# Second convolution layer of a five-layer block: low weight parts made by adding transfers instead of GpSimd subtractions

## The chip, the core and the metric

The kernel runs on one NeuronCore of a Trainium2 chip. The metric is the device time of one execution in microseconds. The engines are TensorE (PE; its weight loads are listed as PEld), VectorE (DVE), ScalarE (ACT), GpSimd (POOL) and SyncE (SP, which issues most transfers). They run their own instruction streams and meet at semaphores. TensorE runs at 1.2 or 2.4 GHz; the profile shows the granted clock as a share of the higher level.

## What is computed

512 tokens of width 1024 in float32 pass through four mixer layers and then a block of two attentions and a feed-forward. Layers 0 and 3 are the same convolution mixer with different weights; layer 3 is "the second convolution layer" (index `j = 1` in the code).

```
def conformer_conv_mixer(h, w_in, conv_w, conv_b, ln_g, ln_b, w_out):
    proj = h @ w_in                                  # 1024 -> 3 * 2048
    val, glu_gate, z = jnp.split(proj, 3, axis=-1)
    u = val * jax.nn.sigmoid(glu_gate)
    u = causal_depthwise_conv(u, conv_w) + conv_b    # 31 taps
    u = jax.nn.silu(layer_norm(u, ln_g, ln_b))
    return (u * jax.nn.silu(z)) @ w_out
...
mix = (sigmoid(gate_a) * (o_a @ w_branch_a) + sigmoid(gate_b) * (o_b @ w_branch_b))
x = x + mix @ w_out
```

The last two lines are from the attention block; `w_branch_a` and `w_branch_b` are the branch weights of the text.

## The kernel before

**Products.** A float32 product is made of three matmuls of a shorter format (float32r): high part of the weights with high part of the activations, high with low, and low with high. `HH` and `HL` hold the parts of the activations, `WH` and `WL` those of the weights. One product of 128 output columns (`gemm`) is 8 x 3 = 24 matmuls of 128x128 by 128x512.

**Weight chunks.** All weights come in a fixed list of chunks `specs` of up to 1 MB. `load_chunk` (SP) loads chunk i from HBM into a raw buffer, half of `WR`; `split_hi` (ACT) copies each of its two halves, 128 partitions x 1024, to `WH`, which rounds them; `split_lo` (POOL) subtracts, `WL = WR - WH`. `WH` and `WL` have two buffers, so `split_hi` of chunk i waits until PE is done with chunk i-2, and `load_chunk` waits until the low parts of the chunk that had the raw buffer are made. PE waits for the low part of a half (`w_lo`) before its product. A chunk of two runs of 128 columns lies in the buffer as eight strips of 256 columns, each half being eight strips of 128.

**Convolution layer.** `layer_a_tensor`, `_vector`, `_scalar` and `_gpsimd` run 33 slots. In slots 0 to 15 PE makes the gate product (half 1 of the slot's chunk) and then the value product (half 0); in slots 16 to 28 one z product, so that a chunk lasts two slots. In slot s ACT first splits the chunk of slot s+1, then takes the sigmoid of the gate; DVE multiplies value and gate and then runs 16 (later 8) of the 31-tap accumulations into PSUM (`SCALAR_TENSOR_TENSOR ps<-AR,CW,ps`). Four channel tiles are convolved wholly or partly by products on ACT and additions on POOL (`TENSOR_TENSOR AR<-AR`). `conv_plan` deals the taps and additions to the slots. On POOL the split of chunk s+1 stands in slot s ahead of the slot's additions, behind those of the slot before. Of `specs`, the layer has 16 chunks with value and gate, 8 with z and 8 of `w_out`.

**Attention block.** While the pairs of attention heads run, the gate products 0 to 13 pass through one staging tile, `STAGE`, which lies in one of the raw buffers together with probabilities of a pair (`W_FREE`), and go to HBM by `gates_sync`; they come back by `gates_back_sync` and ACT takes their sigmoid. The 8 gate chunks (from `C_GATE`) use only the other raw buffer. The first branch chunk is `C_BR`. After the last gate product (n = 15) ACT copies the attention outputs into `HH` (`s_ohi`), POOL and DVE make `HL` from them, even ones and odd ones (`s_olp`, `s_olv`), and PE starts on the branch weights; DVE makes the odd ones after it has waited for the whole product 15.

Of the kernel before, what the change touches and what calls it, by code (L numbers as in the profile page):

```python
# [51 lines left out]
class Engine:  # L52
# [65 lines left out]
def build_program(nc, x, a_norm, a_w_in, a_conv_w, a_conv_b, a_ln_g, a_ln_b, a_w_out, b_norm,  # L118
# [4 lines left out]
    with ctx:  # L123
# [106 lines left out]
        def layer_a_chunks(j):  # L230
# [3 lines left out]
            for i in range(KE // 2):  # L234
                cols(a_w_in[j], (2 * E + 256 * i, 256), used=(a_z, j, 2 * i + 1))
# [49 lines left out]
        def slot_of(i):  # L285
            return (C_GATE + 1) % 2 if C_GATE < i < C_BR else i % 2

        def raw_slot(i):
            return WR[:, slot_of(i) * 2048:(slot_of(i) + 1) * 2048]

        def halves(tile, i):
# [14 lines left out]

        def load_chunk(sp, i):
# [4 lines left out]
            if before:  # L312
                sp.wait_ge(w_lo, before[-1], len(halves(WR, before[-1])) - 1)
            if i == C_BR:
                sp.wait_ge(u_t, 11, 0, 1)
                sp.wait_ge(s_gout, 13)
            if kind in ("in", "deep"):
# [5 lines left out]
                for n, (c0, width) in enumerate(runs):  # L323
                    sp.dma(dst[:, :, o:o + width], src[:, :, c0:c0 + width]).then_inc(
# [29 lines left out]
        def gemm(pe, i, half, o, gen, last=None):  # L354

            pe.wait_ge(w_lo, i, half)
# [10 lines left out]
        def gemm_tokens(pe, i, part, tb, o, gen):  # L367
            sl = slice(tb * P, (tb + 1) * P)
            for n in range(2):
                pe.wait_ge(w_lo, i, n)  # L370
# [176 lines left out]
        def project_tensor(pe, p, first):  # L547
# [10 lines left out]
            def wait_tile(k):  # L558
                pe.wait_ge(w_lo, c0 + k // 2, k % 2)
# [1114 lines left out]
        s_pe, s_pek, s_c, s_cst, s_gelu, s_ck = (sig(n) for n in ("s_pe", "s_pek", "s_c", "s_cst", "s_gelu", "s_ck"))  # L1674
        s_cs, s_cp, s_cexp, s_ct, s_cev = (sig(n) for n in ("s_cs", "s_cp", "s_cexp", "s_ct", "s_cev"))
        u_s, u_ttr, u_exp, u_sh, u_t, u_ev = (sig(n) for n in ("u_s", "u_ttr", "u_exp", "u_sh", "u_t", "u_ev"))
        u_shp, u_fill, s_gout = sig("u_shp"), sig("u_fill"), sig("s_gout")
# [160 lines left out]
        def compress_tensor(pe, n, src):  # L1838
            w3, src3 = t3(W1[n], 16), t3(src, 2)
            if n == 0:  # L1840
# [4 lines left out]
                op.then_inc(s_pe)  # L1845
# [8 lines left out]
        def compress_rest_tensor(pe, n):  # L1854
            pe.wait_ge(s_pek, n, 15)
            if n:
                pe.wait_ge(s_cst, 0)
            pe.mm(banks[5][:, 0:1], PES[n], ones[:, 0:1], True, True).then_inc(s_c, n, "rest")

        def compress_vector(dve):  # L1860
            dve.wait_ge(s_pe)
# [16 lines left out]
        def compress_rest_vector(dve, n):  # L1878
            dve.wait_ge(s_c, n, "rest")
            dve.copy(small(1, "cst", n), banks[5][:, 0:1]).then_inc(s_cst, n)  # L1880

        def compress_rest_scalar(act, n, *dst):
            for at, (g, o) in enumerate(dst):
                act.wait_ge(s_cst, n)
# [5 lines left out]
        def compressed_tensor(pe, i):  # L1890
            pe.wait_ge(s_ck, 1)
# [99 lines left out]
        def pair_scores_vector(dve, u, i, e):  # L1991
# [6 lines left out]
            elif u.n == 2:  # L1998
                dve.wait_ge(s_ct, 3)
                dve.wait_ge(s_c, "v")  # L2000
                dve.wait_ge(w_lo, C_GATE, 1)
            bias = u.bias[e][:, 0:n][:, ::-1]
            if u.n >= 8 and i:
                dve.wait_ge(u_fill, u.n, i, e)
# [4 lines left out]
        def pair_fill_gpsimd(pool, u):  # L2009

            pool.wait_ge(s_tab[1 if u.n < 10 else 2])
            for i, e in BLOCKS:
                if i:
# [4 lines left out]
                        u_fill, u.n, i, e)  # L2018
# [51 lines left out]
        def pair_weigh_tensor(pe, u, i):  # L2070
# [10 lines left out]
            for m in (1, 0) if i == 1 else (i,):  # L2081
                o = [u.bank[rows_of(e), m * P:(m + 1) * P] for e in range(2)]
                if u.branch == 0:
                    pe.wait_ge(s_ck, 1)
# [12 lines left out]
        def second_tensor(pe):  # L2097
# [45 lines left out]
            pe.wait_ge(s_cst, 1)  # L2143
# [594 lines left out]
```

## Time and profile before

| | us |
|---|---|
| median of 3 runs | 2710.47 |
| lowest, highest | 2709.81, 2712.2 |
| the profiled execution | 2709.93 |
| its span | 2708.2 |
| PE busy in the span | 2598.6 (96%) |
| VectorE busy | 1572.4 (58%) |
| ScalarE busy | 1111.8 (41%) |
| GpSimd busy | 1526.1 (56%) |

Times inside the execution are microseconds from the start of the span. The second convolution layer runs from about 1480 to 1910 us, its slots 0 to 28 from about 1501 to 1790; the branch weights come at about 2240. Of the chain of work that ended last, PE holds 75% and VectorE 17%.

### The profile page before, as it was taken

The numbers are of one execution on the slowest core, as the hardware profiler recorded it, in microseconds if no ns is written. First come the engines' busy times: TensorE is split into PE (matmuls) and PEld (weight loads), VectorE is DVE, ScalarE is ACT, GpSimd is POOL, SyncE is SP. The second block draws the span as 40 slices with busy tenths as digits, with TensorE's granted clock in tenths as the row PEclk, the third lists the DMA queues.
The fourth block names the chain that finished last, engine by engine and source line by source line (L and its number), as shares of the span: only waits on it lengthen the run. The fifth ranks groups of instructions, "written<-read, shape, count | busy, mean of one in ns | idle before, by whom it ended". The sixth has DMA issues, their size and how long they took to land.

```text
span 2708.2 us, 31509 instructions
## 1 busy us (share of the span) xinstructions
PE 2598.6 (96%) x12172; PEld 2094.6 (77%) x12172; DVE 1572.4 (58%) x2509; ACT 1111.8 (41%) x1787; POOL 1526.1 (56%) x846
## 2 busy tenths in 40 slices
PE   8999799999999999999999999989999999999998
PEld 6777687877777777888888777768877677788887
DVE  4999975135865834444441799987488753432202
ACT  3454444334654633222232455444335544332322
POOL 3798856444444355444454589866634537544652
PEclk9999999999999999999999999989999999999999
DMA  4232223544344222333333223122431223232221
GB/s 120 78 91 70 89 70 81 102 95 65 77 78 67 78 78 78 109 94 94 101 101 94 63 78 94 63 77 94 117 109 51 95 94 117 82 109 94 94 105 51
DMA packets 267541, 236.63 MB, mean 87 GB/s; under 512 B 16181, under 2 KB 240655, under 8 KB 267392
## 3 DMA queue, kind: packets, MB, share of 16 engines
q1 hardware_dynamic: 264240, 223.94, 29.9%
q0 software_dynamic: 3152, 10.68, 1.3%
q8 instruction: 97, 1.59, 0.2%
q14 instruction: 52, 0.43, 0.1%
HBM read 228.75 MB, written 5.84 MB: 87 GB/s over the span
## 4 chain that ended last, share of the span: by engine, by line
PE 75%; DVE 17%; ACT 3%; issue 2%; POOL 2%; DMA 1%; DVEq 0%; POOLq 0%; ACTq 0%; SPq 0%
PE ps L64 72%; DVE ps L81 7%; DVE AR L81 4%; PE ps L67 2%; DVE AR L73 2%; DVE HL L81 1%; ACT L70 1%; ACT AR L70 1%; POOL AR L73 1%; POOL WL L73 1%; ACT HT L70 1%; DVE X L73 1%; DVE ST L97 0%; DMA AR<-in_x 0%; POOL HL L73 0%
## 5 line engine op out<-in xcount | busy, mean ns | idle before, releaser
L73 POOL TENSOR_TENSOR WL<-WR,WH 128x1024 fp32r<-128x1024 f32 (+1 forms) x405 | 1006.9, 2508 | 863.9 <-ACT WH L70 863.9
L64 PE MATMUL ps<-HH,WH 128*128 128x512 f32 x3080 | 1231.8, 400 | 29.7 <-POOL WL L73 15.1
L64 PE MATMUL ps<-HH,WL 128*128 128x512 f32 x3080 | 1207.3, 392 | 0.0
L64 PE MATMUL ps<-HL,WH 128*128 128x512 f32 x3080 | 1206.7, 392 | 0.0
L64 PEld LDWEIGHTS ps<-HH,WH 128*128 128x128 f32 x3080 | 583.4, 189 | 174.8 <-issue 40.8
L64 PEld LDWEIGHTS ps<-HL,WH 128*128 128x128 f32 x3080 | 583.6, 189 | 123.4 <-issue 6.7
L64 PEld LDWEIGHTS ps<-HH,WL 128*128 128x128 f32 x3080 | 582.6, 189 | 123.6
L70 ACT ACTIVATE WH<-WR 128x1024 fp32r<-128x1024 f32 (+1 forms) x405 | 403.9, 1046 | 477.0 <-PE ps L64 455.4
L81 DVE SCALAR_TENSOR_TENSOR ps<-AR,CW,ps 128x512 f32<-128x512 f32 x732 | 504.8, 747 | 10.4 <-ACT ps L70 3.0
L70 ACT ACTIVATE AR<-ps 128x512 f32<-128x512 f32 (+3 forms) x265 | 132.4, 523 | 413.7 <-PE ps L64 314.2
L73 DVE TENSOR_TENSOR AR<-AR 128x512 f32<-128x512 f32 (+1 forms) x161 | 226.5, 1436 | 39.3 <-ACT AR L70 37.6
L64 PE MATMUL ps<-AR 128*64 128x128 f32 (+16 forms) x1458 | 222.7, 349 | 17.6 <-DVE AR L81 7.3
L73 POOL TENSOR_TENSOR AR<-AR 128x512 f32<-128x512 f32 x154 | 204.8, 1347 | 32.1 <-ACT AR L70 25.5
L64 PEld LDWEIGHTS ps<-AR 128*128 128x128 f32 (+5 forms) x1458 | 135.2, 170 | 75.8 <-issue 44.4
L73 DVE TENSOR_TENSOR HL<-AR,HH 128x512 fp32r<-128x512 f32 x56 | 76.7, 1381 | 200.9 <-ACT HH L70 200.7
L73 DVE TENSOR_TENSOR AR<-ps,HT 128x512 f32<-128x512 f32 (+1 forms) x70 | 47.7, 686 | 247.9 <-PE ps L64 224.5
L67 PE MATMUL ps<-ident,AR 128*128 128x128 f32 (+2 forms) x496 | 87.2, 309 | 52.3 <-DVE ST L97 33.0
L73 DVE TENSOR_TENSOR AR<-AR,HT 128x512 f32<-128x512 f32 x48 | 69.4, 1447 | 101.8 <-ACT AR L70 101.3
L73 DVE TENSOR_TENSOR X<-X,ps 128x512 f32<-128x512 f32 x48 | 32.4, 682 | 162.7 <-PE ps L64 162.7
L67 PEld LDWEIGHTS ps<-ident,AR 128*128 128x128 f32 (+2 forms) x496 | 67.5, 161 | 72.5 <-issue 53.7
L70 ACT ACTIVATE AR<-AR 128x512 f32<-128x512 f32 (+3 forms) x72 | 41.0, 588 | 199.2 <-DVE AR L73 192.9
L73 DVE TENSOR_TENSOR AR<-ps,AR 128x512 f32<-128x512 f32 (+4 forms) x104 | 67.8, 658 | 93.3 <-PE ps L64 92.7
(167 smaller groups left out, 2008.4 us busy)
## 6 DMA issues: line engine op xcount, KB each, us to landing
WR<-in_a_w_in SPq DMA_DIRECT2D x64, 512.0 KB, 5.1
WR<-in_c_w_in SPq DMA_DIRECT2D x64, 512.0 KB, 5.3
WR<-in_a_w_in SPq DMA_DIRECT2D x16, 1024.0 KB, 5.3
WR<-in_a_w_out SPq DMA_DIRECT2D x16, 1024.0 KB, 4.7
WR<-in_b_w_in SPq DMA_DIRECT2D x16, 1024.0 KB, 8.2
WR<-in_b_w_in SPq DMA_DIRECT2D x32, 512.0 KB, 13.3
WR<-in_w_mlp_in SPq DMA_DIRECT2D x16, 1024.0 KB, 5.4
WR<-in_w_mlp_out SPq DMA_DIRECT2D x16, 1024.0 KB, 4.9
```

The costliest lines, as they stand in the source:

```text
L64: return Op(None if self.e is None else self.e.matmul(o, l, r, start=first, stop=last, skip_group_check=True))
L67: return Op(None if self.e is None else self.e.transpose(o, i, identity))
L70: return Op(None if self.e is None else self.e.activation(o, i, f, **kw))
L73: return Op(None if self.e is None else self.e.tensor_tensor(o, a, b, op))
L81: return Op(None if self.e is None else self.e.scalar_tensor_tensor(o, a, s, b, op0, op1))
```

## The change

1. `summed(i)` is true for the 24 chunks of value, gate and z of the second convolution layer. For these ACT writes, after each high half, also the negative high part: `WL = -WR`, rounded in the same way (`scale=-1.0`). POOL issues a transfer that adds the raw half to it, from SBUF to SBUF. Each half has a semaphore `w_sum` of its own, for even and odd chunks, on which PE and SP wait (`wait_low`).
2. A chunk of two runs of 128 columns now has its halves one behind the other, 4 KB a partition, in the raw buffer and in `WH` and `WL`, in all layers. The z chunks are loaded by two transfers of 128 columns instead of one of 256, in both convolution layers.
3. From `C_BR` on the raw buffers change places: the first branch chunk goes into the buffer of the gate chunks, the second into the one with `STAGE`, and so the wait for the staging tile moves from `C_BR` to `C_BR + 1`. The last two staged gates are stored after the load of `C_BR`. ACT takes the first four gate sigmoids ahead of the split of `C_BR`.
4. Some semaphores of the attention block are merged to make room for the four new ones.

```diff
+    def dma_add(self, o, i):
+        return Op(None if self.e is None else self.e.dma_start(o, i, accum_op=ALU.add))
...
-                cols(a_w_in[j], (2 * E + 256 * i, 256), used=(a_z, j, 2 * i + 1))
+                cols(a_w_in[j], (2 * E + 256 * i, P), (2 * E + 256 * i + P, P), used=(a_z, j, 2 * i + 1))
...
-            return (C_GATE + 1) % 2 if C_GATE < i < C_BR else i % 2
+            return (C_GATE + 1) % 2 if C_GATE < i < C_BR else (i + 1) % 2 if i >= C_BR else i % 2
...
+            if two_runs(i):
+                return [t[:, n * 1024:(n + 1) * 1024].rearrange("p (k c) -> p k c", k=8) for n in range(2)]
...
+        def summed(i):
+            return FIRST_A[1] <= i < FIRST_A[1] + KE + KE // 2
+        def wait_low(eng, i, n):
+            if summed(i):
+                eng.wait_ge(w_sum[i % 2][n], i)
+            else:
+                eng.wait_ge(w_lo, i, n)
...
-            if i == C_BR:
+            if i == C_BR + 1:
                 sp.wait_ge(u_t, 11, 0, 1)
                 sp.wait_ge(s_gout, 13)
...
                     act.act(h, r, ACT.Copy).then_inc(w_hi, i, n)
+                    if summed(i):
+                        act.act(halves(WL, i)[n], r, ACT.Copy, scale=-1.0).then_inc(w_hi, i, n, "low")
...
-                    pool.wait_ge(w_hi, i, n)
-                    pool.tt(l, r, h, ALU.subtract).then_inc(w_lo, i, n)
+                    if summed(i):
+                        pool.wait_ge(w_hi, i, n, "low")
+                        pool.dma_add(l.rearrange("p k c -> p (k c)"), r.rearrange("p k c -> p (k c)")).then_inc(w_sum[i % 2][n], i, by=16)
+                    else:
+                        pool.wait_ge(w_hi, i, n)
+                        pool.tt(l, r, h, ALU.subtract).then_inc(w_lo, i, n)
...
-            split_hi(act, C_BR)
             for n in GATES_BACK[0]:
                 act.wait_ge(s_gin[0], "gate", GATES_BACK[0][-1])
                 act.act(GT[n], GT[n], ACT.Sigmoid).then_inc(s_gs, n)
+            split_hi(act, C_BR)
...
-            for n in (2 * m, 2 * m + 1) if m < 5 else range(10, 14) if m == 5 else ():
+            for n in (2 * m, 2 * m + 1) if m < 5 else (10, 11) if m == 5 else (12, 13) if m == 6 else ():
```

POOL's queue in slots 3 to 7 of the second convolution layer, before (`WL<-WR,WH` are the subtractions of a chunk's two halves, `AR<-...` the additions of the convolution):

```order
L73 TENSOR_TENSOR AR<-AR 128x512 x4
L73 TENSOR_TENSOR AR<-AR,SQ 128x512 x2
L73 TENSOR_TENSOR WL<-WR,WH 128x8x128 x2
L73 TENSOR_TENSOR AR<-AR,DG 128x512
L73 TENSOR_TENSOR AR<-AR 128x512 x4
L73 TENSOR_TENSOR WL<-WR,WH 128x8x128 x2
L73 TENSOR_TENSOR AR<-AR,SQ 128x512 x2
```

and now:

```order
L73 TENSOR_TENSOR AR<-AR 128x512 x4
L73 TENSOR_TENSOR AR<-AR,SQ 128x512 x2
L115 DMA WL<-WR 128x1024 x2
L73 TENSOR_TENSOR AR<-AR,DG 128x512
L73 TENSOR_TENSOR AR<-AR 128x512 x4
L115 DMA WL<-WR 128x1024 x2
L73 TENSOR_TENSOR AR<-AR,SQ 128x512 x2
```

The two issues stand where the two subtractions stood, behind the same additions; the second pair here is the one of the chunk of slot 6.

ACT's queue at the same place, before (`AR<-ps` alone is the sigmoid of a gate, `AR<-ps,VB` an evacuation, `AR<-AR,CW` products for POOL):

```order
L70 ACTIVATE ps<-AR,CW 128x512
L70 ACTIVATE AR<-ident,CW 128x128 x2
L70 ACTIVATE DG<-AR,CW 128x512
L70 ACTIVATE AR<-AR,CW 128x512 x4
L70 ACTIVATE WH<-WR 128x8x128 x2
L70 ACTIVATE AR<-ps 128x512
```

and now:

```order
L70 ACTIVATE ps<-AR,CW 128x512
L70 ACTIVATE AR<-ident,CW 128x128 x2
L70 ACTIVATE DG<-AR,CW 128x512
L70 ACTIVATE AR<-AR,CW 128x512 x4
L70 ACTIVATE WH<-WR 128x1024
L70 ACTIVATE WL<-WR 128x1024
```

Each half has its high copy and then its negative copy, four instructions ahead of the next sigmoid instead of two.

SP's queue around the branch weights (`gate_rows<-WR` stores a staged gate, `AR<-gate_rows` fetches some back), before:

```order
L115 DMA WR<-in_w_in 128x8x256
L115 DMA gate_rows<-WR 128x512 x2
L115 DMA AR<-gate_rows 128x512 x4
L115 DMA gate_rows<-WR 128x512
L115 DMA AR<-gate_rows 128x512 x3
L115 DMA gate_rows<-WR 128x512
L115 DMA WR<-in_w_branch_a 128x4x512
L115 DMA AR<-gate_rows 128x512 x3
L115 DMA WR<-in_w_branch_b 128x4x512
```

and now:

```order
L118 DMA WR<-in_w_in 128x8x256
L118 DMA gate_rows<-WR 128x512 x2
L118 DMA AR<-gate_rows 128x512 x4
L118 DMA WR<-in_w_branch_a 128x4x512
L118 DMA gate_rows<-WR 128x512
L118 DMA AR<-gate_rows 128x512 x3
L118 DMA gate_rows<-WR 128x512
L118 DMA WR<-in_w_branch_b 128x4x512
L118 DMA AR<-gate_rows 128x512 x3
```

The load of the first branch chunk has moved ahead of the last two stores, that of the second ahead of the last three fetches. ACT's queue there, as one piece of the difference:

```order
 L70 ACTIVATE AR<-ps 128x512 x2
 L70 ACTIVATE AR<-ps 128x384 x4
+L70 ACT_TABLE_LOAD
+L70 ACTIVATE AR<-AR 128x512 x4
 L70 ACTIVATE WH<-WR 128x4x256 x2
-L70 ACT_TABLE_LOAD
-L70 ACTIVATE AR<-AR 128x512 x4
 L70 ACTIVATE HH<-AR 128x512 x8
```

The table load and the four sigmoids now stand ahead of the split of the branch chunk. PE's and VectorE's queues are the same in both kernels.

## Rows read from the trace of the kernel before

**Rows 1.** The page, section 1: engine, busy us, share, instructions.

```profile
PE 2598.6 (96%) x12172; PEld 2094.6 (77%) x12172; DVE 1572.4 (58%) x2509; ACT 1111.8 (41%) x1787; POOL 1526.1 (56%) x846
```

**Rows 2.** Busy time by stretch: PE, PEld, DVE, ACT, POOL, clock, DMA share, GB/s.

```profile
1600.00:1700.00 100.00, 100.00 (x426) 78.77 (x426) 93.58 (x154) 53.45 (x85) 92.75 (x61) 1.00 0.30 85
1700.00:1820.00 120.00, 102.24 (x430) 80.84 (x430) 110.72 (x200) 56.16 (x81) 83.82 (x54) 0.90 0.21 71
```

**Rows 3.** Chain that ended last, in the layer: start us, us, what.

```profile
1723.47 10.93 PE ps L64 x48
...
1761.91 12.57 DVE ps L81 x20
```

**Rows 4.** Timeline of slots 25 and 26, POOL and PE: start, us, what, idle before.

```profile
1765.58 4.78 POOL L73 TENSOR_TENSOR WL<-WR,WH 128x1024 fp32r<-128x1024 f32 x2
...
1771.63 0.39 PE L64 MATMUL ps<-HH,WH 128*128 128x512 f32 x1
```

**Rows 5.** Issues on POOL by the line that issues: duration ns min/median/max.

```profile
L115 POOL DMA_DIRECT2D AR<-negc_rows x16: 577/577/579, 573.3 to 919.8; - x16
```

**Rows 6.** Timeline, ACT in slot 2.

```profile
1530.05 1.99 ACT L70 ACTIVATE WH<-WR 128x1024 fp32r<-128x1024 f32 x2
```

**Rows 7.** Timeline, PE in slots 3 and 6, DVE in slot 3.

```profile
1536.97 0.39 PE L64 MATMUL ps<-HH,WH 128*128 128x512 f32 x1
...
1549.98 0.69 DVE L73 TENSOR_TENSOR AR<-ps,AR 128x512 f32<-128x512 f32 x1
...
1576.61 0.77 PE L64 MATMUL ps<-HH,WH 128*128 128x512 f32 x1 [6.40 <-POOL WL L73]
```

**Rows 8.** Transfers on POOL's queue: count, KB each, median us from issue to landing.

```profile
AR<-negc_rows POOLq DMA_DIRECT2D x16, 256.0 KB, 4.5
...
AR<-bias_by_distance POOLq DMA_DIRECT2D x1, 2048.0 KB, 8.5
AR<-bias_by_distance POOLq DMA_DIRECT2D x2, 1024.0 KB, 7.3
...
negc_rows<-AR POOLq DMA_DIRECT2D x1, 32.0 KB, 3.7
```

**Rows 9.** Timeline, POOL in slots 4 and 5.

```profile
1566.46 5.38 POOL L73 TENSOR_TENSOR AR<-AR 128x512 f32<-128x512 f32 x4
1571.80 4.67 POOL L73 TENSOR_TENSOR WL<-WR,WH 128x1024 fp32r<-128x1024 f32 x2
```

**Rows 10.** Timeline, SP's queue at the first branch chunk.

```profile
2229.84 0.38 SPq L115 DMA_DIRECT2D WR<-in_w_branch_a  x1
```

**Rows 11.** Timeline, ACT at the first branch chunk.

```profile
2224.76 0.87 ACT L70 ACTIVATE AR<-ps 128x384 f32<-128x384 f32 x2 [2.82 <-PE ps L67]
2235.01 2.01 ACT L70 ACTIVATE WH<-WR 128x1024 fp32r<-128x1024 f32 x2 [9.38 <-DMA WR<-in_w_branch_a]
2237.04 1.28 ACT L70 ACT_TABLE_LOAD   x1
2238.34 2.19 ACT L70 ACTIVATE AR<-AR 128x512 f32<-128x512 f32 x4
2240.43 4.26 ACT L70 ACTIVATE HH<-AR 128x512 fp32r<-128x512 f32 x8
```

**Rows 12.** Timeline, POOL and DVE there.

```profile
2206.70 4.96 POOL L73 TENSOR_TENSOR WL<-WR,WH 128x1024 fp32r<-128x1024 f32 x2 [15.93 <-ACT WH L70]
2236.15 4.72 POOL L73 TENSOR_TENSOR WL<-WR,WH 128x1024 fp32r<-128x1024 f32 x2 [24.49 <-ACT WH L70]
...
2241.67 6.35 DVE L73 TENSOR_TENSOR HL<-AR,HH 128x512 fp32r<-128x512 f32 x4 [8.02 <-ACT HH L70]
```

**Rows 13.** Timeline, PE's first matmuls on the branch weights.

```profile
2242.54 0.77 PE L64 MATMUL ps<-HH,WH 128*128 128x512 f32 x1 [4.18 <-POOL HL L73]
2243.10 0.63 PE L64 MATMUL ps<-HH,WL 128*128 128x512 f32 x1
...
2248.65 0.40 PE L64 MATMUL ps<-HL,WH 128*128 128x512 f32 x1
```

More of the change, by code:

```diff
@@ L285, in slot_of, with two_runs @@
         def slot_of(i):
-            return (C_GATE + 1) % 2 if C_GATE < i < C_BR else i % 2
+            return (C_GATE + 1) % 2 if C_GATE < i < C_BR else (i + 1) % 2 if i >= C_BR else i % 2
         def raw_slot(i):
             return WR[:, slot_of(i) * 2048:(slot_of(i) + 1) * 2048]
+        def two_runs(i):
+            return specs[i][0] == "in" and [n for _, n in specs[i][2]] == [P, P]
         def halves(tile, i):
@@ L305, in build_program @@
         w_hi, w_lo = sig("w_hi"), sig("w_lo")
+        w_sum = [[sig(f"w_sum{i}{n}") for n in range(2)] for i in range(2)]
+        def summed(i):
[5 more added lines that the diff above has]
+                eng.wait_ge(w_lo, i, n)
         def load_chunk(sp, i):
@@ L312, in load_chunk @@
             if before:
-                sp.wait_ge(w_lo, before[-1], len(halves(WR, before[-1])) - 1)
-            if i == C_BR:
+                wait_low(sp, before[-1], len(halves(WR, before[-1])) - 1)
+            if i == C_BR + 1:
                 sp.wait_ge(u_t, 11, 0, 1)
@@ L323, in load_chunk @@
                 for n, (c0, width) in enumerate(runs):
-                    sp.dma(dst[:, :, o:o + width], src[:, :, c0:c0 + width]).then_inc(
+                    to = halves(WR, i)[n] if two_runs(i) else dst[:, :, o:o + width]
+                    sp.dma(to, src[:, :, c0:c0 + width]).then_inc(
                         w_landed[i % 2], i, n - len(runs), by=16)
@@ L354, in gemm @@
         def gemm(pe, i, half, o, gen, last=None):
-            pe.wait_ge(w_lo, i, half)
+            wait_low(pe, i, half)
             wh, wl = halves(WH, i)[half], halves(WL, i)[half]
@@ L369, in gemm_tokens @@
             for n in range(2):
-                pe.wait_ge(w_lo, i, n)
+                wait_low(pe, i, n)
             for kk in range(4):
@@ L1673, in build_program @@
         s_w2, s_tab = sig("s_w2"), [sig("s_tab_b"), sig("s_tab_a0"), sig("s_tab_a1")]
-        s_pe, s_pek, s_c, s_cst, s_gelu, s_ck = (sig(n) for n in ("s_pe", "s_pek", "s_c", "s_cst", "s_gelu", "s_ck"))
+        s_pek, s_c, s_gelu = (sig(n) for n in ("s_pek", "s_c", "s_gelu"))
         s_cs, s_cp, s_cexp, s_ct, s_cev = (sig(n) for n in ("s_cs", "s_cp", "s_cexp", "s_ct", "s_cev"))
         u_s, u_ttr, u_exp, u_sh, u_t, u_ev = (sig(n) for n in ("u_s", "u_ttr", "u_exp", "u_sh", "u_t", "u_ev"))
-        u_shp, u_fill, s_gout = sig("u_shp"), sig("u_fill"), sig("s_gout")
+        u_shp, s_gout = sig("u_shp"), sig("s_gout")
         s_gin = [x_in, small_in, sig("s_gin"), sig("stored")]
@@ L1879, in compress_rest_vector @@
             dve.wait_ge(s_c, n, "rest")
-            dve.copy(small(1, "cst", n), banks[5][:, 0:1]).then_inc(s_cst, n)
+            dve.copy(small(1, "cst", n), banks[5][:, 0:1]).then_inc(s_pek, "cst", n)
         def compress_rest_scalar(act, n, *dst):
             for at, (g, o) in enumerate(dst):
-                act.wait_ge(s_cst, n)
+                act.wait_ge(s_pek, "cst", n)
                 act.wait_ge(consts, "s_zero", n)
@@ L2163, in gate_part_tensor @@
                 if 0 in rows:
-                    pe.wait_ge(w_lo, i, half)
+                    wait_low(pe, i, half)
                     if n:
@@ L2204, in second_tensor @@
                 wh, wl = halves(WH, i)[half], halves(WL, i)[half]
-                pe.wait_ge(w_lo, i, half)
+                wait_low(pe, i, half)
                 for k in range(8):
@@ L2225, in second_tensor @@
                             pe.wait_ge(u_ev, 11, 1, n - 2)
-                        pe.wait_ge(w_lo, i, half)
+                        wait_low(pe, i, half)
                         for k in range(4):
@@ L2300, in second_vector @@
             dve.wait_ge(s_c, "k")
-            dve.copy(CK, banks[4][:, 0:64]).then_inc(s_ck, 0)
+            dve.copy(CK, banks[4][:, 0:64]).then_inc(s_pek, "ck", 0)
             dve.wait_ge(s_c, "v")
-            dve.copy(CV, banks[5][:, 0:128]).then_inc(s_ck, 1)
+            dve.copy(CV, banks[5][:, 0:128]).then_inc(s_pek, "ck", 1)
             index_vector(dve, 3, range(4, 8))
@@ L2329, in second_vector @@
                 if n == 0:
-                    dve.wait_ge(w_lo, C_GATE, 1)
+                    wait_low(dve, C_GATE, 1)
                 else:
```

24 lines of the change are left out of this document (12 added, 12 removed).

## The prediction

> **What bounds the kernel now.** I read the page's busy shares first, then the stretches of the second convolution layer, then the chain of work that ended last, and only then single instructions. TensorE (PE) is busy 96% of the span [rows 1], so elsewhere than in a few stalls nothing can be won by relieving another engine. The stretches of the second convolution layer show who shares the bound there: from 1600 to 1700 us PE is busy 100.00 of 100 us and VectorE (DVE) 93.58; from 1700 to 1820 us PE has fallen to 102.24 of 120 while DVE is busy 110.72 [rows 2]. PE sets the middle of the layer and DVE its head and tail. GpSimd (POOL), whose work the change takes away, has 36 us free in the last of these stretches [rows 2]. In the chain PE's products carry the middle of the layer (10.93 us for 48 matmuls at 1723.47) and DVE's taps the tail, 12.57 us in one piece at 1761.91 [rows 3].
>
> **The change, part by part.** *Work removed and added in the second convolution layer.* 24 chunks of two halves lose 48 POOL subtractions: two take 4.78 us [rows 4], so 24 x 4.78 = 115 us of POOL. POOL gets 48 issues of a transfer, 0.577 us each by the row of the 16 issues that are nearest in size [rows 5], 28 us. ScalarE (ACT) gets 48 more copies. A pair takes 1.99 us [rows 6], so 48 us in all, or 2.0 us per chunk. All this lies off the path unless it comes late: the relief of POOL is worth nothing in itself, since nobody waits for POOL except for the low weights at 1576.61 [rows 7]. So what counts is when the low half is ready. Before: ACT's pair, then POOL's pair. After: four ACT copies (4.0 us), the issue, and the time from issue to landing, which I call L.
>
> *L.* No row shows a transfer that adds, nor one from SBUF to SBUF. Issued on POOL's queue, 256 KB landed after 4.5 us, 1024 KB after 7.3 and 2048 KB after 8.5 [rows 8]. A half is 512 KB: on the line through the first two, 4.5 + (7.3 - 4.5)/3 = 5.4 us. It must also read its destination, which costs something up to a doubling of the bytes, 7.3 us; and two halves are often issued back to back, 2 MB of reads together, 8.5 us. Against that, 32 KB between SBUF and HBM took 3.7 us [rows 8], which is the lower end. I take 6.0, near the plain 5.4, and keep 3.7 and 8.5.
>
> The Trainium skill (DMA: Bandwidth & Descriptors, section Anatomy of one DMA) gives 2.0 us plus bytes/436 GB/s for a transfer issued by GpSimd. Its page Collectives: The Full Stack (section Putting both ceilings together and the part before it) says that a reduce moves at half the rate of a copy since it needs two source reads. By both, a half would be an estimated 2.0 + 2.4 us plus its issue, 5.0 us, and the sum below would end about 2 us lower. No run here shows either yet.
>
> *Where L is not hidden.* In slot 2 ACT's pair for the chunk of slot 3 starts at 1530.05 [rows 6]; four copies end at about 1534.1, and L = 6.0 puts the half that PE needs first at 1540.1. PE began that product at 1536.97 [rows 7]: 3.1 us late. Two products (48 matmuls) take 10.93 us [rows 3], so they end at 1551.0 rather than 1547.9, and DVE, which multiplies with the result at 1549.98 [rows 7] and is the bound here, waits 1.1 us. The slots before it have more room. For the chunk of slot 6, POOL starts the subtraction at 1571.80 because its additions (5.38 us for four) end there [rows 9]; that queue does not get shorter, for it hangs on ACT and on DVE. Shifted by 1.1, the second issue is at 1571.80 + 1.1 + 0.58 = 1573.5, it lands at 1579.5, and PE starts at 1579.6 instead of 1576.61 [rows 7]: +3.0 us. This contains the 1.1. From there to about 1690 PE is the bound, so the 3.0 stay.
>
> Further on each chunk has room. The tightest that matters is that of slot 26: POOL is free at 1765.58 and PE needs the chunk at 1771.63 [rows 4], 6.0 us. Six more chunks measured in the same way have 6.4 (three), 6.7, 7.2 and 7.6; all others have 8 or more, or 10 us of idle PE behind them. With L = 6.0 none of them stalls. ACT's two extra microseconds stand ahead of the evacuations of the z products, and one of these releases PE: 0.4 us. **Sum of the layer: +3.4 us.** With L = 3.7 it is -0.4 + 0.4 = 0.
>
> *Raw buffers from the branch weights on.* Here the trace shows a stall that goes away. Before, the first branch chunk is loaded at 2229.84 [rows 10], into the buffer that holds the gate staging. ACT waits 9.38 us for it, copies it by 2237.02, loads a table for 1.28 us, takes four sigmoids and starts the high copies of the attention output at 2240.43 [rows 11]; POOL and, at 2241.67, DVE [rows 12] follow with the low ones, and PE, idle for 4.18 us, restarts at 2242.54 [rows 13]. It restarts at the lower of its two clock levels: matmuls of 0.77 us and then of 0.63, until they take 0.40 us from 2248.65 on [rows 13].
>
> After, the chunk goes into the other buffer, free when POOL's subtraction of 2206.70 ends at 2211.66 [rows 12], so it has landed by about 2217. ACT, free at 2225.63 [rows 11], does table (1.28), sigmoids (2.19) and the pair (2.01): 2231.1. POOL's pair runs 2230.1 to 2235.0 and its first low copy (6.35/4 = 1.59 us by DVE's row beside it, [rows 12]) is there at 2236.6, before PE is free at 2242.54 - 4.18 = 2238.36. What is late next is DVE: its odd low copies wait for the whole last gate product, so they come at 2240.0 and 2241.6, and PE's first twelve matmuls end at 2242.3. The 13th starts there instead of two steps of 0.43 before 2248.65, that is 2247.8; two more steps at the full rate against the low one add 0.4. **Gain 5.9 us.** It is 3.1 if the two pauses of under 2 us still drop the clock (14 matmuls, 0.43 against 0.23 us a step) and 6.5 if DVE's copies run faster, POOL being done. The second branch chunk, now in the staging buffer, is issued at 2229.84 as the first was, and PE comes to it 3 x 2.73 us later, at 2250.5; hidden.
>
> *Layout, split z loads, merged semaphores.* The halves of two 128-column runs become contiguous. The subtraction takes 2.4 us each in both layouts, by the pair of 4.78 on halves of eight strips [rows 4] and of 4.72 on other halves [rows 12]; zero. 16 chunk loads become two issues with 512-byte rows; a pair of such loads is what the val and gate chunks use already, and nobody waits for them; zero. Merging semaphores moves no instruction; zero.
>
> **Total:** 3.4 - 5.9 = -2.5 us. The profiled execution of 2709.93 us (span 2708.2) would become 2707.4. It lies 0.54 us under the median of the three runs, 2710.47, so the median would become **2708.0 us**. A measurement of this kernel tells about 0.2% (5.4 us) from no change.
>
> **The rivals.** *A: the transfer is slow, and the kernel gets slower.* Mechanism: PE waits in every tight slot for a landing. It decides from L = 7.3 on. At L = 8.5: slot 3 costs DVE 3.6 us; slot 6 starts at 1572.4 + 3.6 + 8.5 + 0.1 = 1584.6, +8.0; the seven chunks add 7 x 8.5 - (6.0 + 3 x 6.4 + 6.7 + 7.2 + 7.6) = 12.8; with 0.4 that is +21.2, less 5.9: 2725.8 us. Each further microsecond costs about nine. For it: an add reads twice, two halves share the DMA engines, and 1024 KB alone took 7.3 us on POOL's queue [rows 8]. Against it: both ends are SBUF, and rows are 4 KB long. Chance 0.30.
>
> *B: the transfer is short.* L under 4.4: the layer costs nothing, and the gain at the branch weights stands alone, -5.5 to -6.5: 2704.5 us. For it: the 3.7 us row, and the longer ones all read or write HBM. Chance 0.20.
>
> *C: the change does not bring its earlier load,* since something else holds PE at 2238 (DVE's odd copies, the clock): gain 3.1, sum +0.3, 2710.8 us. It counts as no change. Chance 0.07.
>
> *D: POOL does not come free at the issue* but holds until landing. Its row of 0.577 us against 4.5 us to landing [rows 5, 8] speaks against it; it would end in A's range and is in its chance.
>
> **How the numbers follow.** Forecast 0.43, C 0.07, B 0.20, A 0.30. The forecast's own range is L from 4.4 to 7.2, 2705.0 to 2715. The whole range goes from B's best with a little more, 2702.5, to a bit over A at L = 8.5, 2730; about 2 in 10 is left, most above. Faster by over 0.2% means B: 0.21. Slower means A: 0.30. Within: 0.49.
>
> **What would show it.** Right: landings of the adding transfer at 5 to 7 us; PE idle before the gate product of slot 6 a little over the present 6.4 us; no other wait of PE for the low weights after 1600 us; PE's gap of 4.18 us at the branch weights gone, with matmuls at 0.39 us there. Wrong: landings over 7.3 us with a wait in each gate slot; or POOL's issue over 1 us; or ACT, busier by 48 us, in the chain.

## The result, and the profile after

The changed kernel took 2717.22 us (median of 11 runs, 2709.36 to 2719.29), the kernel before 2709.81 us in the same comparison. The ratio is 1.0022, with a 95% interval of 1.0013 to 1.0030: slower by a little over 0.2%. A second comparison of the same two kernels gave 2714.63 against 2710.37 us, ratio 1.0015 (1.0006 to 1.0024). The forecast was 2708.0 us and no measurable change. The single case with the sign that came out was rival A, a slow transfer. It isn't what happened in the main: in the profile 4 of the 48 transfers took 7.3 us or more.

The profiled execution took 2712.3 us (span 2710.6), 2.4 us more than the profiled one of before. The page's sections 1, 3 and 6 show what moved:

```profile
PE 2602.8 (96%) x12172; PEld 2095.4 (77%) x12172; DVE 1575.5 (58%) x2509; ACT 1157.4 (43%) x1835; POOL 1454.1 (54%) x846
...
q0 software_dynamic: 10064, 35.85, 6.2%
...
WL<-WR POOLq DMA_DIRECT2D x48, 512.0 KB, 5.6
```

GpSimd (POOL) lost 72 us against [rows 1] (115 us of subtractions went, and the profile books 0.86 us for each of the 48 issues), ScalarE (ACT) got 46, and TensorE (PE) is as busy as it was. The adding transfers land 5.6 us after their issue in the median.

Two stretches answer to [rows 2] (busy us of PE, PEld, DVE, ACT, POOL, then granted clock, DMA share and GB/s). PE is still without a gap from 1600 to 1700, and the DMA share is two to three times what it was:

```profile
1600.00:1700.00 100.00, 100.00 (x427) 78.77 (x426) 93.19 (x149) 66.64 (x99) 66.10 (x58) 1.00 0.73 162
1700.00:1820.00 120.00, 102.05 (x433) 81.34 (x433) 114.61 (x210) 69.95 (x99) 66.84 (x59) 0.90 0.63 147
```

**Where the time went.** PE runs the same 12,172 matmuls in the same order in both kernels, so each can be compared with its twin. In the two profiled executions the changed kernel stands 1.6 us behind from 953 us on, a stretch that the change doesn't touch: there PE ran at half its rate a little longer. The rest has three parts. It loses 3.1 us from 1478 to 1500 us, ahead of the layer; 4.0 us in slots 1 to 6 of the layer; and it gains 6.4 us at the branch weights.

*Ahead of the layer.* Before, ACT made the high parts of the layer's first chunk while PE finished the projection of the layer ahead, and then squared the residual for the normalisation. Its timeline (start us, us, instruction, idle before) in the kernel before:

```profile
1475.57 2.01 ACT L70 ACTIVATE WH<-WR 128x1024 fp32r<-128x1024 f32 x2 [8.87 <-PE ps L64]
1477.59 0.63 ACT L70 ACTIVATE SQ<-X 128x512 f32<-128x512 f32 x1
```

The same place after:

```profile
1477.17 1.06 ACT L70 ACTIVATE WH<-WR 128x1024 fp32r<-128x1024 f32 x1 [8.87 <-PE ps L64]
1478.14 1.04 ACT L70 ACTIVATE WL<-WR 128x1024 fp32r<-128x1024 f32 x1
1479.09 1.04 ACT L70 ACTIVATE WH<-WR 128x1024 fp32r<-128x1024 f32 x1
1480.03 1.04 ACT L70 ACTIVATE WL<-WR 128x1024 fp32r<-128x1024 f32 x1
1480.98 1.13 ACT L70 ACTIVATE SQ<-X 128x512 f32<-128x512 f32 x2
```

The two negating copies stand ahead of the squares. PE, whose queue has the column sums of the squares between its products, waits for the first square and comes back at half its rate (0.63 us a matmul against 0.39; one starts every 0.43 us instead of every 0.23):

```profile
1481.65 1.09 PE L64 MATMUL ps<-ones,SQ 128*128 128x1 f32 x8 [1.85 <-ACT SQ L70]
1482.60 0.78 PE L64 MATMUL ps<-HH,WH 128*128 128x512 f32 x1
1483.17 0.63 PE L64 MATMUL ps<-HL,WH 128*128 128x512 f32 x1
```

These copies are on the chain of work that ended last (start us, us, what), as the prediction's list of signs against it had it ("ACT, busier by 48 us, in the chain"):

```profile
1477.17 1.06 ACT WH L70
1478.23 0.95 ACT WL L70
1479.18 0.94 ACT WH L70
1480.13 0.95 ACT WL L70
1481.07 0.53 ACT SQ L70
```

*In the layer.* PE waits for adding transfers five times; the view of waits gives us in total, times, longest. Before, POOL's low weights cost one wait of 6.40 us [rows 7]:

```profile
PE ps L64 <- DMA WL<-WR: 9.1, 5, 5.7
```

The timeline of PE shows three of them, the first products of slots 1, 2 and 6 (slots 4 and 5 wait 0.41 and 0.47):

```profile
1521.75 0.50 PE L64 MATMUL ps<-HH,WH 128*128 128x512 f32 x1 [1.66 <-DMA WL<-WR]
...
1533.83 0.47 PE L64 MATMUL ps<-HH,WH 128*128 128x512 f32 x1 [0.90 <-DMA WL<-WR]
...
1585.18 0.76 PE L64 MATMUL ps<-HH,WH 128*128 128x512 f32 x1 [5.68 <-DMA WL<-WR]
```

*At the branch weights.* [rows 10, 11, 13] have these counterparts on SP's queue, ACT and PE. The load is issued while ACT is still at the attention, ACT's table load and sigmoids no longer wait behind it, and PE's gap of 4.18 us is one of 0.28, three matmuls into the branch weights, at the full clock:

```profile
2220.52 0.38 SPq L118 DMA_DIRECT2D WR<-in_w_branch_a  x1
...
2234.47 1.28 ACT L70 ACT_TABLE_LOAD   x1
2235.76 2.20 ACT L70 ACTIVATE AR<-AR 128x512 f32<-128x512 f32 x4
2237.86 1.99 ACT L70 ACTIVATE WH<-WR 128x1024 fp32r<-128x1024 f32 x2
2242.45 5.39 ACT L70 ACTIVATE HH<-AR 128x512 fp32r<-128x512 f32 x8 [2.60 <-PE ps L64]
...
2248.13 0.50 PE L64 MATMUL ps<-HH,WH 128*128 128x512 f32 x1 [0.28 <-DVE HL L73]
```

The sum of these explains 2.4 us between two profiles, but not 4 to 7 us between two medians. The experiments had to price each part by itself and find what the profile had missed.

### The profile page after: what moved, and what is told of

It is laid out like the page before. It is cut to its first block, busy times and chain, and to the rows that moved or that the text cites. A ratio compares the mean times of both kernels' runs of the same rounds, so it can differ in the third digit from the quotient of the medians.

```text
span 2710.6 us, 31587 instructions
## 1 busy us (share of the span) xinstructions
PE 2602.8 (96%) x12172; PEld 2095.4 (77%) x12172; DVE 1575.5 (58%) x2509; ACT 1157.4 (43%) x1835; POOL 1454.1 (54%) x846
## 4 chain that ended last, share of the span: by engine, by line
PE 76%; DVE 15%; ACT 3%; issue 2%; POOL 2%; DMA 1%; DVEq 0%; POOLq 0%; ACTq 0%
PE ps L64 74%; DVE ps L81 6%; DVE AR L81 4%; PE ps L67 2%; DVE AR L73 2%; DVE HL L81 1%; ACT L70 1%; ACT AR L70 1%; POOL AR L73 1%; ACT HT L70 1%; POOL WL L73 1%; DVE X L73 1%; DMA WL<-WR 1%; DVE ST L97 0%; DMA AR<-in_x 0%
## 5 line engine op out<-in xcount | busy, mean ns | idle before, releaser
L73 POOL TENSOR_TENSOR WL<-WR,WH 128x1024 fp32r<-128x1024 f32 (+1 forms) x357 | 893.2, 2524 | 837.7 <-ACT WH L70 837.7
```

Of the source, the lines that this page charges most:

```text
L73: return Op(None if self.e is None else self.e.tensor_tensor(o, a, b, op))
```

## The experiments

Ratios are to the kernel before on the same chip; the widths of their intervals are about 0.2%, or 5 us. Kernels are built from the changed one where nothing else is said.

**Each part by itself.** Four kernels first. `swap_only` is the kernel before with `slot_of`, the wait moved to `C_BR + 1`, the sigmoids ahead of `split_hi(act, C_BR)` and the new `gates_sync`:

```
-return (C_GATE + 1) % 2 if C_GATE < i < C_BR else i % 2
+return (C_GATE + 1) % 2 if C_GATE < i < C_BR else (i + 1) % 2 if i >= C_BR else i % 2
```

> The kernel before with the exchange of the two weight buffers at the branch weights alone (and the order of loads, sigmoids and row transfers that goes with it); no adding transfer, no new layout. The working theory, from the two traces: TensorE's matmuls after the branch weights stand 6.4 us nearer to those of before than ahead of them (offset 8.85 us at 1804.96, 2.4 us at 2251), so the exchange by itself is worth 6.4 us: 2703.4 us, ratio 0.9976, and the idle stretch of 4.18 us at 2242.54 is gone. Rival: the gain exists only because the layer ahead ended later and so gave the first branch load a different start; then this kernel stays within 1.5 us of 2709.8 and a wait on the branch weights is back.

Measured 2704.72 us, ratio 0.9977 (0.9966 to 0.9987). The exchange is worth 5.7 us without the rest, 5.9 being forecast; the rival falls.

`adds_no_swap` is the other half of the change: the changed kernel with all lines of the exchange as they were before.

> The changed kernel with the weight buffers at the branch weights as they were before the change; the adding transfers, the halves in one piece and the split z loads stay. The working theory (each late start that the two traces show, priced by them): 3.1 us where ScalarE's copies of the layer's first chunk stand ahead of the squares of the residual, and 4.0 us of waits for low halves in the first seven slots, 7.1 us together: 2716.9 us, ratio 1.0026. Rival: the two traces are not typical of most runs, and the transfers also cost about 5 us by a lower clock that the profiled run did not show; then 2722 us or more, ratio 1.0045, with a granted clock that is lower in a stretch without any wait for a low half.

Measured 2717.82 us, ratio 1.0029 (1.0020 to 1.0038); in single runs 2715.5 to 2725.9. The median is the first theory's. But its profiled run took 2725.9 us, and there PE lost 9.5 us from 1478 to 1500, not 3.1.

`neg_only` is the kernel before with the negating copies added, GpSimd subtracting as before:

```
 act.act(h, r, ACT.Copy).then_inc(w_hi, i, n)
+if FIRST_A[1] <= i < FIRST_A[1] + KE + KE // 2:
+    act.act(halves(WL, i)[n], r, ACT.Copy, scale=-1.0).then_inc(w_hi, i, n, "low")
```

> The kernel before, with ScalarE's 48 negating copies added and nothing else: GpSimd waits for them and then subtracts as before, over what they wrote. The working theory: the copies cost 3.1 us at the layer's first chunk, as in the changed kernel, and little in the slots (GpSimd's subtraction starts 1 to 2 us later; its tightest room before was at slots 3 and 6, where 2 us are at stake): 2713 to 2715 us, ratio 1.0012 to 1.002. Rival: all of the layer's cost is the latency of the transfers, and the copies fit beside other work, as the prediction had it: 2710 to 2711 us.

Measured 2714.73 us, ratio 1.0017 (1.0008 to 1.0025). The copies aren't hidden. But the profiled execution (2714.49 us) shows the same gap of PE without any half rate behind it:

```profile
1482.53 1.05 PE L64 MATMUL ps<-ones,SQ 128*128 128x1 f32 x8 [1.85 <-ACT SQ L70]
...
1483.76 0.39 PE L64 MATMUL ps<-HL,WH 128*128 128x512 f32 x1
```

The gap cost this execution 1.5 us. It stood 2.5 us behind before it, by places that the copies don't touch.

`skip0` leaves the layer's first chunk to GpSimd's subtraction:

```
-return FIRST_A[1] <= i < FIRST_A[1] + KE + KE // 2
+return FIRST_A[1] < i < FIRST_A[1] + KE + KE // 2
```

> The changed kernel, but the layer's first chunk has its low halves by GpSimd's subtraction, as before; 23 chunks are still summed by transfers. The working theory: the two negating copies of that chunk (1.9 us of ScalarE from 1478.14) held the square of the residual's first part back, TensorE idled 1.85 us and came back at half its rate, and the normalisation ended 3.1 us late. Without them the column sums start as before and the kernel is 3.1 us faster than the changed one: 2714.1 us against 2717.2. Rival: the late start there belongs to the other ways in which the two runs differ (an offset of 1.6 us was there since 953), and the layer's first gate product stays 4.7 us late: 2717 us.

Measured 2709.89 us, ratio 0.9996 (0.9987 to 1.0005): not 3 but 5 to 7 us faster than the changed kernel. The place was right and the price too small.

**Which copies, which transfers.** `neg0_only` is `neg_only` for the first chunk alone (`if i == FIRST_A[1]`).

> The kernel before, with ScalarE's two negating copies added for the layer's first chunk alone (GpSimd subtracts over them, as before). The working theory: these two instructions of 1.04 us carry the whole price of the 48: 2714.7 us as with all of them (ratio 1.0017), with TensorE's first column sum 1.9 us late and a stretch at half its rate behind it. Rival: the price lies in the slots, where GpSimd starts 1 to 2 us later, and this kernel stays within 1 us of 2710.4.

Measured 2713.4 us, ratio 1.0014 (1.0005 to 1.0023), against 1.0017 with all 48. Within the measurement two of the 48 copies carry the whole price; the other 46, 46 us of ACT's work, are hidden. Its profile agrees: 3.2 us are lost at the gap and 0.4 in all the rest.

`from7` has transfers from the eighth chunk on (`FIRST_A[1] + 7 <= i < ...`), and `no_adds` has none (`return False`), but the new layout, the split loads and the exchange.

> The changed kernel with the adding transfers from the layer's eighth chunk on only (17 of 24 chunks); the first seven have GpSimd's subtraction. The working theory: from slot 7 on nothing waits for a low half, so the transfers there are free and worth nothing either: the time is that of the exchange at the branch weights alone, 2704.7 us (ratio 0.9977). Rival: the transfers also cost where nobody waits for them, by slowing weight loads and by ScalarE's 34 copies of 1 us, and the time is 2707 us or more; or GpSimd's free time (some 80 us) is worth something, and it is under 2702.

> The changed kernel without any adding transfer and without negating copies: the halves in one piece, two loads for each z chunk and the exchange at the branch weights stay. The working theory: layout and split loads cost nothing, 2704.7 us (ratio 0.9977) as the exchange alone. Rival: 16 more loads on SP's queue, or copies between tiles with other strides, cost or bring 1 us or more.

Measured: `from7` 2703.64 us, ratio 0.9974 (0.9965 to 0.9983); `no_adds` 2703.93 us, ratio 0.9978 (0.9970 to 0.9987). Layout and split loads cost nothing, as forecast. And 34 of the 48 transfers, with 81 us less of GpSimd's subtractions, neither cost nor bring anything. Both of these, and `swap_only`, beat the kernel before (the upper ends of their intervals are 0.9983 to 0.9987), and with it the changed one.

`from2` has transfers from the third chunk on.

> The changed kernel with the adding transfers from the third chunk on (22 of 24); the first two have GpSimd's subtraction. The working theory, from the waits in the traces: of the 6.0 us that lie between 2709.9 (23 chunks summed) and 2703.9 (none), slot 1 holds about 4: a wait of 2.0 us for its low half and 1.8 us at half the rate behind it; slots 4 and 5 hold 1.0 each: 2705.8 us (ratio 0.9983). Rival: with slot 1 on time, slots 2 to 5 stall in its place, each chunk's transfer being 1 to 2 us later than a subtraction: 2709 us.

Measured 2706.49 us, ratio 0.9986 (0.9977 to 0.9995). By the medians 2.6 us over `no_adds` are left to chunks 2 to 6, and 3.4 us lie between this kernel and `skip0`, by the theory the price of slot 1. Its profile is less simple: slots 1 and 2 are cheap there, and PE waits 1.95 us in slot 3 instead, as the rival had it.

**The order on ACT.** `squares_first` sums all 24 chunks, but moves the first chunk's two negating copies:

```
 for k in range(KD):
     square(act, 1, k)
+    if k in (1, 2):
+        negate(act, FIRST_A[1], k - 1)
```

> The changed kernel with all 24 chunks summed by transfers, but the two negating copies of the first chunk stand behind the squares of the residual's second and third part, where ScalarE idles 2.0 and 1.65 us, instead of ahead of the first square. The working theory: the first column sum starts as before, TensorE keeps its full rate, and the time falls to that of the kernel without copies for the first chunk, 2709.9 us (ratio 0.9996). Rival: the first chunk's price was its transfers or the later copies' effect on the normalisation, not the order on ScalarE; then it stays at 2714 to 2717 us.

Measured 2707.34 us, ratio 0.9991 (0.9982 to 1.0000). ACT's timeline in it: the square follows the high copies again, and the first negating copy stands in a pause.

```profile
1476.58 2.01 ACT L70 ACTIVATE WH<-WR 128x1024 fp32r<-128x1024 f32 x2 [8.87 <-PE ps L64]
1478.60 0.63 ACT L70 ACTIVATE SQ<-X 128x512 f32<-128x512 f32 x1
1479.96 0.63 ACT L70 ACTIVATE SQ<-X 128x512 f32<-128x512 f32 x1 [0.73 <-DVE X L73]
1480.50 1.04 ACT L70 ACTIVATE WL<-WR 128x1024 fp32r<-128x1024 f32 x1
```

The same instructions in another order, and the kernel is 7.3 and 9.9 us faster than the changed one by the two medians of that (6.5 and 8.4 us by the ratios). That is the direct test of the cause. The median also gives the layer's own price: with every transfer in place, 3.4 us over `no_adds`. The profiled execution, one of its slower ones (2711.18 us), has 6.4 us there.

**Why 7 us and not 3.** The changed kernel was run again for a second profile.

> The changed kernel again, for a second profile and more times. The working theory: its times fall into two groups, 2709 to 2712 and 2715 to 2719 us, by whether TensorE's clock stays at half for a few microseconds more after the idle stretch of 1.85 us near 1480 (the kernel with the adding transfers and the old buffers lost 8.4 us there in its profile, the changed kernel's first profile 3.1 us). A profile of the upper group then shows an offset of about 8 us against the kernel before by 1490, one of the lower group about 3 us. Rival: the upper group owes its time to another place, such as waits on transfers after 1600; then the offset at 1490 is about 3 us in both groups.

Measured 2714.63 us (2709.11 to 2719.61), ratio 1.0015 (1.0006 to 1.0024); the profiled run was the longest of its runs, 2719.61 us. It has the same gap of 1.85 us and the same half rate behind it (the lower of PE's two clock levels, 1.2 GHz), but this lasts until 1497. In the first profile it was over by about 1486, after six of the large matmuls. The timeline of PE in the second one:

```profile
1478.95 1.36 PE L64 MATMUL ps<-ones,SQ 128*128 128x1 f32 x8 [1.85 <-ACT SQ L70]
1480.17 0.77 PE L64 MATMUL ps<-HH,WH 128*128 128x512 f32 x1
1480.74 0.63 PE L64 MATMUL ps<-HL,WH 128*128 128x512 f32 x1
...
1495.25 0.63 PE L64 MATMUL ps<-HH,WL 128*128 128x512 f32 x1
1495.68 1.39 PE L64 MATMUL ps<-ones,SQ 128*128 128x1 f32 x8
1496.93 0.48 PE L64 MATMUL ps<-HH,WH 128*128 128x512 f32 x1
1497.24 0.39 PE L64 MATMUL ps<-HL,WH 128*128 128x512 f32 x1
```

The stretch of 1480 to 1500 us in it (columns as above) has a granted clock of 0.59, where the first profile of the changed kernel has 0.90:

```profile
1480.00:1500.00 20.00, 20.00 (x76) 17.29 (x77) 3.43 (x5) 3.15 (x5) 0.00 (x0) 0.59 0.37 86
```

Against its twins in the kernel before, PE loses 9.5 us there instead of 3.1: it stood 1.1 us ahead before the gap and 8.4 us behind at 1500. Nine profiles have this gap. The loss there is 1.5 us in one (`neg_only`), 3.1 or 3.2 in three (the first of the changed kernel, `neg0_only`, `neg0_adds1`), and 9.5 in five (the second of the changed kernel, `adds_no_swap`, `quarters`, `sum0_only`, `neg0_swap`). So one gap has three prices, and the last two are 6.3 us apart.

The second profile differs in the layer too. In slot 1 PE waits 2.66 us for the adding transfer and then drops to half its rate from 1527.3 to 1530.7, which costs 1.7 us more; in the first profile it did not:

```profile
1526.39 0.50 PE L64 MATMUL ps<-HH,WH 128*128 128x512 f32 x1 [2.66 <-DMA WL<-WR]
...
1527.94 0.63 PE L64 MATMUL ps<-HH,WL 128*128 128x512 f32 x1
```

The slots 0 to 28 cost 7.7 us in this execution and 4.1 in the first. So this profile adds up as well: -1.1 before the layer, +9.5, +7.7, -6.3 at the branch weights, 9.8 us together, and the execution took 9.7 us more than the profiled one of before.

The gap is the larger part of the spread of the changed kernel's 22 runs, 2709.1 to 2719.6 us. In the first comparison they lie in two groups, four up to 2712.3 and seven from 2715.3 on; in the second the border isn't sharp. That the groups are the two prices is inferred from the profiles; a run without one doesn't show its gap.

What makes the half rate last? The adding transfers of the first chunk run beside these very matmuls. Three kernels separate the two. `neg0_adds1` makes the first chunk's copies in their place but subtracts on GpSimd, and sums the other 23 chunks; `sum0_only` has `return i == FIRST_A[1]`; `neg0_swap` is `neg0_only` with the exchange at the branch weights, and has no adding transfer at all.

> The changed kernel, the first chunk's negating copies in their place ahead of the squares, but its low halves by GpSimd's subtraction over them; the other 23 chunks are summed by transfers. Theory 1, the transfers of the first chunk, running beside the matmuls after the idle stretch, make the half-rate stretch long: without them only 3 us are lost, 2709.9 + 3.0 = 2713 us and a single profile offset of 2 to 4 us by 1490. Theory 2, the long stretch comes by chance after the idle stretch alone: 2714.6 to 2717.2 us as the changed kernel, with times in two groups.

> The changed kernel with the adding transfers in the first chunk alone; 23 chunks have GpSimd's subtraction. Theory 1: the two transfers bring the long half-rate stretch in most runs, 8 us behind the kernel without any: 2703.9 + 7 = 2711 us (ratio 1.0003). Theory 2: as the kernel with the idle stretch and no transfer at all (neg0_swap), whatever that is, within 1 us.

> The kernel before with the exchange at the branch weights and ScalarE's two negating copies for the first chunk; no adding transfer. Theory 1: the idle stretch of 1.85 us and a short stretch at half rate, 2703.9 + 3.0 = 2706.9 us (ratio 0.9989). Theory 2: the idle stretch alone costs what it costs in the changed kernel, 2711 us (ratio 1.0003).

Measured:

| kernel | median | 11 runs, in their two groups | ratio |
|---|---|---|---|
| neg0_adds1 | 2714.88 us | 2710.9 to 2719.6, no clear gap | 1.0016 (1.0007 to 1.0025) |
| sum0_only | 2712.27 us | 5 at 2706.5 to 2708.5, 6 at 2712.3 to 2713.8 | 0.9998 (0.9989 to 1.0007) |
| neg0_swap | 2708.92 us | 6 at 2706.4 to 2708.9, 5 at 2712.8 to 2716.4 | 0.9998 (0.9989 to 1.0007) |

The profile of `neg0_swap`, a kernel without any adding transfer, settles it. It has the same gap, matmuls of 0.63 us, and a granted clock of 0.57 from 1480 to 1500 us. Its timeline of PE:

```profile
1479.41 1.37 PE L64 MATMUL ps<-ones,SQ 128*128 128x1 f32 x8 [1.85 <-ACT SQ L70]
1480.65 0.77 PE L64 MATMUL ps<-HH,WH 128*128 128x512 f32 x1
1481.22 0.63 PE L64 MATMUL ps<-HL,WH 128*128 128x512 f32 x1
```

And its stretch:

```profile
1480.00:1500.00 20.00, 20.00 (x77) 17.38 (x77) 3.43 (x5) 2.73 (x5) 1.76 (x1) 0.57 0.19 52
```

Theory 1, that the transfers beside the matmuls keep the clock low, falls, though it was right on the median of `sum0_only` within 1.3 us. The gap alone can do it, for a short time, for a long time, or not at all. What decides stays open. In the nine profiles it goes with the time at which PE came back: 1478.8 to 1479.4 us in the five long ones, 1479.8 to 1481.7 in the three short ones, 1482.5 in the one without half rate. No run moves that time by itself, so this is a pattern and not a shown cause. The share is open too: by the times 5 of 11 runs of `neg0_swap` are long, but only one of 11 of `neg0_only` (2719.07 us, the others 2711.6 to 2714.6), which differs from it 740 us later. With 11 runs each, that difference may be chance.

**What a transfer takes.** In `held`, transfers from the eighth chunk on, each weight load waits until the transfers of the chunk ahead have landed:

```
+if summed(i - 1):
+    for n in range(2):
+        wait_low(sp, i - 1, n)
```

> Transfers from the eighth chunk on, and each weight load there is held until the adding transfers of the chunk ahead have landed, so that no load runs beside one. Landing times are what is looked at. The working theory: a half alone takes 4.5 us and one issued 0.6 us behind another 6.5; all landings of 6.6 to 9.1 us were those beside a 1 MB weight load, and are gone: none over 6.8. The time rises by some 25 us, since load, copies and transfers then follow one another (14 us a chunk against 10.9 us of products). Rival: the long landings come from the state of the transfers themselves (their number, GpSimd's load), and some over 7.2 us remain.

The line of the adding transfers in `held`, the shortest, the median and the longest time from issue to landing:

```profile
DMA to landing us min/median/max: 4.5/5.4/6.7
```

In the changed kernel:

```profile
DMA to landing us min/median/max: 4.5/5.6/8.5
```

In the traces of the other kernels all landings over 8 us (up to 9.5, in `from2` and the second profile of the changed kernel) have a weight load beside them, and in `held` there are none. A load beside it doesn't always slow a transfer: the changed kernel has some at 4.6 us that were issued late in a load. Holding the loads also spread the halves, most of them 1.9 us apart, where the other kernels have many at 0.58, so `held` doesn't test the load alone. One transfer per execution, near slot 14, took 7.0 to 8.0 us without a load beside it in most profiles; what slows it stays open. The time, one run of 2740.69 us, rose by 37 and not 25 us over `from7`: a chunk took 15.4 us, not 14.

`quarters` sums each half by two transfers of 256 KB:

> The changed kernel with each half summed by two transfers of 256 KB. The working theory: a transfer costs about 1.9 us fixed and 2.6 us for 512 KB, and the fixed part overlaps that of the one behind it; the first quarter lands after about 3.3 us, the second 4.6 us after the first was issued, so a half is as late as in one transfer, and the time is that of the changed kernel, 2714.6 to 2717.2 us. Rival: each transfer's fixed part, or its issue (0.58 us of GpSimd), comes on top; a half is then 0.6 to 2 us later and slots 1 to 5 lose 0.6 to 2 us each: 2719 us or more.

```profile
DMA to landing us min/median/max: 3.3/4.9/7.7
```

Measured 2716.19 us, ratio 1.0021 (1.0012 to 1.0031), as the changed kernel; its ten runs lie in two groups, five at 2712.1 to 2713.8 us and five at 2718.6 to 2719.5. The shortest landing is 3.3 us for 256 KB and 4.5 for 512 KB. The line through these two gives an estimate of 2.1 us fixed and 1.2 us for each 256 KB. In time, twice as many issues cost nothing that can be measured.

## Why the prediction was wrong, point by point

**The step that failed** is the first of the part on the layer: "All this lies off the path unless it comes late: (...) So what counts is when the low half is ready." It priced ACT's 48 us only through the arrival of the low halves. It didn't ask what else stands behind the new copies on ACT, and for the first chunk that is the square for which PE waits. The chunk's copies are not in the layer's slots but ahead of its normalisation, a place that no row of the prediction covers. By the profiles this missing term, which the prediction had at nothing, is 1.5 us without the half rate, 3.1 when that is short and 9.5 when it is long. Between the medians of `squares_first` and the changed kernel it is 7 to 10 us. None of the four rivals held it: A has the right sign, but by a landing of 7.3 us or more in general, and it measured 5.6 in the median. That the time lies inside the range stated for all cases is luck, since no case in it had this term.

**The sum of the layer, +3.4 us,** was low: 3.4 us by the medians of `squares_first` and `no_adds`, but 6.0 by `skip0`, 4.1 in the first profile, and 6.4 to 7.7 in five other profiles with all chunks from slot 1 on summed by transfers (second of the changed kernel, `adds_no_swap`, `skip0`, `squares_first`, `neg0_adds1`). Part of the miss is PE's half rate behind the waits, which the sum had at nothing. Its places were wrong too. It had slots 1 and 2 with "more room" and put the delay at slots 3 and 6. But by its own terms slot 1 was late too. The timelines of ACT and of PE in the kernel before:

```profile
1507.43 1.98 ACT L70 ACTIVATE WH<-WR 128x1024 fp32r<-128x1024 f32 x2
```

```profile
1515.21 0.39 PE L64 MATMUL ps<-HH,WH 128*128 128x512 f32 x1
```

Four copies from 1507.43 end at 1511.4, and with L = 6.0 the half lands at 1517.4: 2.2 us late. In the first profile slot 1 waited 1.66 us, in the second 2.66, and since PE was the bound there, all of it stayed. Slot 3 then had no wait in the first profile and 0.30 us in the second, for PE was already late. At slot 6 PE waited 5.68 us, less than the 6.40 of before, instead of "a little over".

**L, taken at 6.0,** was the right size: 5.6 us in the median, 4.5 for a half alone and 6.5 for one issued 0.6 us behind. The upper bound of 8.5 was reached in the first profile and passed in the second (9.5), beside a weight load. What was wrong is that L was one number: it was 4.5 to 9.5 us in one kernel, and the longest all stood beside a load of the next chunk. By the Trainium skill (DMA: Bandwidth & Descriptors, section Anatomy of one DMA, with Collectives: The Full Stack, section The bandwidth ceiling, on a reduce that reads two sources) a half was an estimated 5.0 us with its issue, 4.4 without. The trace agrees with the latter for a half alone, 4.5 us counted from the start of the issue.

**After 1600 us** the prediction had no stall, and the first profile shows none. The second shows a wait of 0.64 us at 1682.11, `squares_first` one of 0.50 at 1673.06 and `from7` one of 0.99 at 1665.02. All three stand behind that transfer near slot 14 (7.6, 7.5 and 8.0 us).

**GpSimd's relief worth nothing:** right. `from7` takes 34 subtractions off it and gains nothing that can be measured. Its issue, taken as 0.577 us, is booked at 0.86 in the profile, but two in a row do follow each other by 0.58.

**Branch weights, a gain of 5.9 us:** right: 5.7 us in `swap_only`, 6 to 7 us in `no_adds` and `from7`, 6.3 to 6.4 us in the profiles. PE went on at its full rate (0.40 us a matmul) behind the pause of 0.28 us, so rival C, a gain of 3.1 us, was not the case.

**Layout, split loads, merged semaphores at zero:** right for layout and split loads (`no_adds` 0.9978, `swap_only` 0.9977). The merged semaphores are in `no_adds` and not in `swap_only`, so they cost nothing either.

Together, by the medians: -6 for the branch weights, +3.4 to +6 for the layer, and +7 to +10 for two copies ahead of it. That is 4 to 10 us, and the two comparisons gave 7.4 and 4.3. The prediction had the first term, had the second low, and lacked the third.

## What to carry to other kernels

When work moves to another engine, list what stands behind every new instruction on that engine's queue, at the first and the last instance above all: 46 of the 48 copies were free, and the two that stood ahead of a value PE waited for cost more, by the medians, than all transfers together. A gap of PE has no fixed price: 1.85 us of waiting cost 1.5, 3.1 or 9.5 us, since the half rate behind it is absent, short or long, and one profile shows only one of the three. So judge a change of a few microseconds by its runs, and take a second profile where medians and trace disagree.

## What the runs showed of the hardware

- Behind the same idle stretch of 1.85 us PE's matmuls took 0.63 us until about 1486 in one execution of the changed kernel and until 1497 in another, and in `neg_only` they took 0.39 us at once. It isn't the adding transfers' doing: `neg0_swap` has none and was at 0.63 us until 1497 too.
- A transfer from SBUF to SBUF that adds took 4.5 us at the least for 512 KB, 3.3 us for 256 KB, and up to 9.5 us for 512 KB beside a weight load from HBM (two transfers of 512 KB). With loads held back none took more than 6.7 us.
- GpSimd issued the next such transfer 0.58 us after the first, with 4.5 us to the first one's landing; it doesn't wait for it.
